# Delta-rule scan: level copies under a mask, and crossed row halves for the second unit of a group

## The chip, the cores and the metric

The program runs on one core of a Trainium2 chip. The metric is the device time of one execution in microseconds; the median of 3 runs of the kernel before is 5740.78 us (5734.3 to 5745.99).

## The reference

The program is a chain of blocks over 2048 tokens (plus 256 of context): a mixing block with a pooling branch, a delta-rule (RWKV) branch and a gated linear (HGRN) branch, and two attention blocks. The change concerns the delta-rule recurrence alone, which the reference computes token by token for 6 heads of 64 and 2 directions:

```python
def step(S, inp):
    w_t, k_t, v_t, kk_t, a_t = inp[:5]
    sa = jnp.einsum('bhvk,bhk->bhv', S, kk_t)
    S = (S * w_t[:, :, None, :] - sa[..., None] * (kk_t * a_t)[:, :, None, :]
         + v_t[..., None] * k_t[:, :, None, :])
    y = jnp.einsum('bhvk,bhk->bhv', S, inp[5]) if emit else None
    return S, y
```

The kernel computes it in chunks of 64 tokens. Within a chunk the recurrence is a triangular system, so a chunk needs the inverse of a unit triangular 64 × 64 matrix I − A; the state then moves from chunk to chunk with dense products.

## The kernel before

`rwkv_scan` (L1415 to L1740) is one stage of the program, with a barrier of all engines before and after it (`Scope.close`). It goes through 18 steps of 128 tokens, 2 of context and 16 that emit outputs. In a step there are 6 *units* (`u`: three pairs of heads times two directions) in 3 *groups* (`g`, two units each). A unit holds 128 tokens, two chunks of 64, each on one half of the 128 rows (`CHUNKS`), and two heads (`HEADS`). All loops are unrolled in Python, so TensorE's instructions are one long list.

A step has the phases of `PHASES` (L1428), and in each phase the three groups come in turn (`walk`, L1468):

- **z** and **n**, five levels of doubling (blocks of 2 up to 64). `W` holds the inverse so far and its transpose, started by GpSimd (L1535) from the identity plus level 0. In z (L1593 to L1597) TensorE multiplies the level's part of A with one of them and ScalarE copies the result to `K_Z` (L1683). In n (L1606 to L1613) TensorE multiplies that with the other, in both orders, and VectorE subtracts the products from `W` (L1715). The level's part of A comes from GpSimd, which multiplies A with six level masks `lv` for every unit (L1532). At level 1 the z phase also multiplies `K_KL` with `K_V` (L1599 to L1603).
- **x** (L1614): the inverse times two operands at once, 128 columns wide; ScalarE negates it into `X12` (L1686).
- **p** (L1621): the chunk's transition (`pq`) and its contribution and local output (`gram`), evacuated by VectorE (L1721) and ScalarE (L1689). The group's products for `pq` wait until VectorE has emptied `pq` of the group before, those for `gram` until ScalarE has.
- **f** and **s** (L1650): the state through the first and the second chunk, added up by VectorE (L1731, L1734).

Every matmul of z, n and x reads rows `t` (one chunk's half) and writes rows `t`:

```python
last = mm(d[t, at:at + HD], tk[t, K_LB + lev, u, HEADS[h]], wt[t, u, 0, HEADS[h]])
```

so unit 0 and unit 1 both use the array's quarters (rows 0, columns 0) and (rows 64, columns 64), and all their results lie in one PSUM bank per group (`db`, 512 columns). The products of p read rows `CHUNKS[cp]` and write rows `HEADS[h]` in the order of `LANES`, which visits all four quarters; `pq` and `gram` have two banks each, one for each row half read. `tb` is the bank of the transposes.

The work for the next step's units is put between the phases (`AHEAD`, L1429): after n of each of the five levels and after x, `front` (L1562) makes four transposes of a unit into `tb` (copied by ScalarE, L1676) and its 12 gram products into `gram` (multiplied by a mask into `TK`, VectorE, L1706). Before that GpSimd scales the unit's inputs (L1521, L1523). SP loads a unit's five arrays of the step after next with one DMA (L1495), in the p phase of the step that uses the buffer last, and stores outputs in s (L1501). The constants, the level masks among them, are loaded at the stage's start (L1481), and every engine waits for all five.

Of the kernel before, what the change touches and what calls it, by code (L numbers as in the profile page):

```python
# [1414 lines left out]
def rwkv_scan(nc, R, E, masks, levels, eye, ident, YR):  # L1415
# [8 lines left out]
    K_AL, K_BE, K_KA, K_V, K_A, K_AR, K_KL, K_KR, K_AT, K_LB, K_Z, K_W0 = 0, 1, 2, 3, 4, 5, 6, 7, 8, 9, 15, 16  # L1424
# [4 lines left out]
    AHEAD = {1: 0, 3: 1, 5: 2, 7: 3, 9: 4, 10: 5}  # L1429
# [3 lines left out]
    with ExitStack() as ctx:  # L1433
# [3 lines left out]
        TK = [[s.sb(f"TK{b}{g}", [P, 17, 2, P]) for g in range(NG)] for b in range(2)]  # L1437
# [6 lines left out]
        mk = s.sb("mk", [P, 2, 5, C])  # L1444
        lv = s.sb("lv", [P, 2, LV, P])
# [9 lines left out]
        xe_ready, tl_full, tl_done, gram_full, m4_done, lb_part, lb_ready = (  # L1455
            s.sem(n) for n in ("xe_ready", "tl_full", "tl_done", "gram_full", "m4_done", "lb_part", "lb_ready"))
# [11 lines left out]
        def walk(k, b, emit, phase, front):  # L1468

            nxt = after(k, b)  # L1470
            for i, (w, lev) in enumerate(PHASES):
                for g in range(NG):
                    phase(k, b, emit, w, lev, g)
                if nxt and i in AHEAD:
                    front(*nxt, AHEAD[i])

        with nc.Block() as block:
            @block.sync
            def _(sp):
                for dst, src in ((mk, masks), (lv, levels), (ey, eye), (idn, ident), (e, E)):  # L1480
                    sp.dma_start(dst[:], src).then_inc(const_in, 16)  # L1481
                for b in range(2):
                    for u in range(NU):
                        m, d = divmod(u, 2)
                        c = NLT + b if d == 0 else NS - 1 - b
                        sp.dma_start(X[b][u][:, X_AL:, :], R[c, m, d]).then_inc(x_in[b][u], 16)

                def step(k, b, emit):
                    if k < NLT // 2:
                        for u in range(NU):  # L1490
# [4 lines left out]
                            sp.dma_start(X[b][u][:, X_AL:, :], R[c, m, d]).then_inc(x_in[b][u], 16)  # L1495
# [12 lines left out]
            def _(pool):  # L1508
# [4 lines left out]
                def scaled(k, b, u):  # L1513
# [3 lines left out]
                    pool.wait_ge(x_in[b][u], k * 16 + 16)  # L1517
# [9 lines left out]
                def levels_of(k, b, u):  # L1527
# [4 lines left out]
                    nc.gpsimd.tensor_tensor(tk[:, K_LB:K_LB + LV, d, :], tk[:, K_A:K_A + 1, d, :].broadcast_to([P, LV, P]), lv[:, d, :, :],  # L1532
                                            ALU.mult).then_inc(lb_part, 1)
                    pool.wait_ge(lb_part, f + 1)
                    nc.gpsimd.tensor_tensor(W[b][g][:, d, :, :], tk[:, K_AT:K_LB + 1, d, :], ey[:].unsqueeze(1).broadcast_to([P, 2, P]),  # L1535
                                            ALU.add).then_inc(lb_ready, 1)

                def fronts(k, b):
                    scaled(k, b, 0)
                    scaled(k, b, 1)  # L1540
                    for u in range(NU):
                        levels_of(k, b, u)
                        if u + 2 < NU:
                            scaled(k, b, u + 2)
# [10 lines left out]
            def _(pe):  # L1555
# [6 lines left out]
                def front(k, b, u):  # L1562
# [3 lines left out]
                    begun = f > 0  # L1566
                    pe.wait_ge(xe_ready, f + 1)
                    if begun:
                        pe.wait_ge(tl_done, f)
                    for j, src in enumerate((x[:, X_AL, :], XE[u % 2][:, 0, :], XE[u % 2][:, 1, :], x[:, X_V, :])):  # L1570
                        t = nc.tensor.transpose(tb[:, j, :], src, idn[:])
                    t.then_inc(tl_full, 1)
                    if begun:
                        pe.wait_ge(m4_done, f)
                    for a, at in ((X_BE, 0), (X_KA, 2 * C)):
                        for cp, h in LANES:
                            mm(gram[CHUNKS[cp], h, at:at + 2 * C], x[HEADS[h], a, CHUNKS[cp]], x[HEADS[h], X_AL:X_RH + 1, CHUNKS[cp]])
                    for cp, h in LANES:
                        last = mm(gram[CHUNKS[cp], h, 4 * C:5 * C], x[HEADS[h], X_AL, CHUNKS[cp]], x[HEADS[h], X_BE, CHUNKS[cp]])
                    last.then_inc(gram_full, 1)  # L1580

                def phase(k, b, emit, w, lev, g):

                    tk, wt, d = TK[b][g], W[b][g], db[g]
# [2121 lines left out]
```

## Time and profile before

| | us |
|---|---|
| Median of 3 runs | 5740.78 |
| The profiled execution, its own time | 5741.89 |
| Its span, first to last instruction | 5740.1 |
| TensorE busy | 5142.9 |
| VectorE busy | 3334.5 |
| GpSimd busy | 1634.3 |

The profiled execution is 1.1 us above the median of the runs. Its span leaves 1.8 us of its own time outside. Busy times are for the whole program; the scan is the stretch from 1061 to 1857 us. In the rows, PE is TensorE's matmuls and PEld its weight loads, DVE VectorE, ACT ScalarE, POOL GpSimd, SP the engine that issues loads. An fp32 matmul leaves two records of each kind. "issue" is time in which an engine waited for nothing that the profile shows.

### The profile page before, as it was taken

The page shows a single profiled execution, that of the slowest core. Times are in us where ns is not written, and L with a number is a line of the kernel's source. Part 1 is how long each engine was busy: PE and PEld are TensorE (multiplying, and loading weights), DVE is VectorE, ACT ScalarE, POOL GpSimd, SP SyncE. Part 2 cuts the span into 40 slices and gives each one's busy share as a digit, 9 for nine tenths or more (in the row PEclk, how much of TensorE's full clock was granted, in tenths as well). Part 3 has the DMA queues.
Part 4 walks back from the last instruction along what each step waited for, and adds up shares of the span by engine and source line. Part 5 has one row for each costly group of instructions (what it writes and reads, how often), then busy time and mean ns, then how long its engine had stood idle before and what let it go on. Part 6 is the DMA issues. An engine that isn't in the chain of part 4 may idle for free. (4 is left out here: it accounts for less than half of the span.)

```text
span 5740.1 us, 122226 instructions
## 1 busy us (share of the span) xinstructions
PE 5142.9 (90%) x52673; PEld 3953.4 (69%) x52673; DVE 3334.5 (58%) x5037; ACT 1880.5 (33%) x3105; POOL 1634.3 (28%) x1351
## 2 busy tenths in 40 slices
PE   6899999899998786697999769999987999979989
PEld 1588888788888675485888534444466888766667
DVE  2237556344444777494995358888855100158877
ACT  1324444333332552224111314444412100126652
POOL 2201111444443441135000007777734311000012
PEclk8999999899999898898999879999998999979999
DMA  6334444312111112454332420000075211220035
GB/s 204 121 113 149 150 145 147 110 50 68 55 53 50 59 55 102 172 176 121 105 112 79 186 89 19 18 18 18 19 211 161 78 70 70 101 105 33 32 123 163
DMA packets 429687, 560.77 MB, mean 98 GB/s; under 512 B 66838, under 2 KB 318742, under 8 KB 417262
## 3 DMA queue, kind: packets, MB, share of 16 engines
q1 hardware_dynamic: 361480, 373.28, 21.0%
q10 hardware_dynamic: 52470, 122.50, 5.6%
q0 software_dynamic: 15216, 57.44, 2.5%
q8 instruction: 401, 6.57, 0.5%
q14 instruction: 120, 0.98, 0.1%
HBM read 350.00 MB, written 203.12 MB: 96 GB/s over the span
## 5 line engine op out<-in xcount | busy, mean ns | idle before, releaser
L157 PE MATMUL p_bank<-p_hT_high,p_w_high 128*128 128x512 f32 (+1 forms) x2744 | 1037.1, 378 | 7.9 <-PEq L37 7.9
L159 PE MATMUL p_bank<-p_hT_high,p_w_low 128*128 128x512 f32 (+1 forms) x2744 | 1028.9, 375 | 0.0
L158 PE MATMUL p_bank<-p_hT_low,p_w_high 128*128 128x512 f32 (+1 forms) x2744 | 1028.9, 375 | 0.0
L157 PEld LDWEIGHTS p_bank<-p_hT_high,p_w_high 128*128 128x128 f32 x2744 | 517.0, 188 | 110.1 <-issue 17.6
L159 PEld LDWEIGHTS p_bank<-p_hT_high,p_w_low 128*128 128x128 f32 x2744 | 516.8, 188 | 93.3
L158 PEld LDWEIGHTS p_bank<-p_hT_low,p_w_high 128*128 128x128 f32 x2744 | 517.2, 188 | 91.4
L2951 POOL TENSOR_TENSOR at_acc<-at_acc,at_p 128x512 f32<-128x512 f32 x256 | 415.1, 1622 | 122.8 <-ACT at_p L2887 99.8
L2887 ACT ACTIVATE at_p<-at_sc 128x1024 f32<-128x1024 f32 (+1 forms) x296 | 284.7, 1013 | 377.4 <-PE at_sc L2778 371.9
L1560 PE MATMUL rsc_db<-rsc_W,rsc_TK 64*64 64x64 f32 x8640 | 385.7, 220 | 4.6 <-issue 4.0
L2993 DVE TENSOR_REDUCE at_mx<-at_mb 128x2 f32<-128x1024 f32 (+1 forms) x280 | 342.1, 1222 | 50.7 <-PE at_mb L2789 50.4
L157 PE MATMUL o_bank<-o_w_high,o_m_high 128*128 128x512 f32 x800 | 314.7, 393 | 63.3 <-POOL o_m_low L151 63.3
L1560 PEld LDWEIGHTS rsc_db<-rsc_W,rsc_TK 64*64 64x64 f32 x8640 | 357.5, 137 | 5.2 <-issue 4.5
L158 PE MATMUL o_bank<-o_w_low,o_m_high 128*128 128x512 f32 x800 | 313.7, 392 | 0.0
L159 PE MATMUL o_bank<-o_w_high,o_m_low 128*128 128x512 f32 x800 | 313.5, 392 | 0.0
L1028 DVE COPY p_o<-p_bank 128x512 f32<-128x512 f32 (+1 forms) x52 | 33.8, 651 | 465.1 <-PE p_bank L159 465.1
L1715 DVE TENSOR_TENSOR rsc_W<-rsc_W,rsc_db 128x512 f32<-128x512 f32 x270 | 171.4, 635 | 208.8 <-PE rsc_db L1560 207.2
L1532 POOL TENSOR_TENSOR rsc_TK<-rsc_TK,rsc_lv 128x768 f32<-128x768 f32 x108 | 196.0, 1814 | 331.8 <-DVE rsc_TK L1706 331.8
L2810 PE MATMUL at_ob<-at_p,at_V 128*64 128x512 f32 (+1 forms) x1184 | 283.3, 599 | 0.7 <-ACT at_osb L2894 0.7
L1560 PE MATMUL rsc_db<-rsc_TK,rsc_W 64*64 64x64 f32 (+1 forms) x4320 | 258.4, 228 | 0.6 <-issue 0.6
L2777 PE MATMUL at_sc<-at_Q,at_K 128*128 128x512 f32 (+1 forms) x592 | 247.5, 419 | 1.8 <-DMA at_Q<-attention_tops 1.8
L406 ACT COPY p_o<-p_bank 128x512 f32<-128x512 f32 (+1 forms) x147 | 82.2, 560 | 476.7 <-PE p_bank L159 468.3
L3025 DVE TENSOR_TENSOR at_acc<-at_acc,at_p 128x512 f32<-128x512 f32 x256 | 204.2, 798 | 55.8 <-ACT at_p L2887 49.5
(428 smaller groups left out, 10401.2 us busy)
## 6 DMA issues: line engine op xcount, KB each, us to landing
rsc_X<-rwkv_chunks SPq DMA_DIRECT2D x108, 320.0 KB, 4.6
pT<-p_o ACTq DMA_DIRECT2D x128, 256.0 KB, 2.2
rwkv_chunks<-p_arr POOLq DMA_DIRECT2D x54, 512.0 KB, 5.4
o_z<-pT SPq DMA_DIRECT2D x50, 512.0 KB, 5.3
o_y<-y SPq DMA_DIRECT2D x50, 512.0 KB, 6.6
pT<-p_eo ACTq DMA_DIRECT2D x96, 256.0 KB, 2.0
x<-o_o ACTq DMA_DIRECT2D x32, 512.0 KB, 2.8
o_x<-x SPq DMA_DIRECT2D x32, 512.0 KB, 4.6
```

The costliest lines, as they stand in the source:

```text
L157: nc.tensor.matmul(out, lhs[0], rhs[0], start=start, stop=False)
L158: nc.tensor.matmul(out, lhs[0], rhs[1], start=False, stop=False)
L159: return nc.tensor.matmul(out, lhs[1], rhs[0], start=False, stop=stop)
L1532: nc.gpsimd.tensor_tensor(tk[:, K_LB:K_LB + LV, d, :], tk[:, K_A:K_A + 1, d, :].broadcast_to([P, LV, P]), lv[:, d, :, :], ALU.mult).then_i ...
L1560: return nc.tensor.matmul(out, l, r, start=start, stop=stop)
L1715: nc.vector.tensor_tensor(wt, wt, d[:].rearrange("p (u a t) -> p u a t", u=2, a=2)[:, :, lo:, :], ALU.subtract).then_inc(evac[g], 1)
L2777: nc.tensor.matmul(sc[t % 2][:, h, 0:n], K1[kv][:, keys], Q1[b % NBUF][:, h, 0:n], start=True, stop=False)
L2810: m = nc.tensor.matmul(ob[h * HD:(h + 1) * HD, 0:n], V[:, tiles[j], kv * HD:(kv + 1) * HD], pr[t % 4][:, h, 0:n], start=(j == 0), stop=(t ...
L2887: nc.scalar.activation(pr[t % 4][:, :, 0:n], sc[t % 2][:, :, 0:n], ACT.Exp, scale=SC).then_inc(exp_done, 1)
L2951: nc.gpsimd.tensor_tensor(acc[b % 2][:, 1, 0:n], acc[b % 2][:, 1, 0:n], pr[t % 4][:, 1, 0:n], ALU.add).then_inc(sum_b, 1)
L2993: r = nc.vector.reduce_max(mx[b % 2][:, :, t:t + nt, c], top_bank(m)[:, :, 0:nt * n].rearrange("p h (j k) -> p h j k", j=nt), AX)
L3025: nc.vector.tensor_tensor(acc[b % 2][:, 0, 0:n], acc[b % 2][:, 0, 0:n], pr[t % 4][:, 0, 0:n], ALU.add).then_inc(sum_a, 1)
```

## The change

- `K_A` gets a minus sign in the gram mask, and z multiplies the whole A with `W` in place of a level's part. What n makes is right only where the level's mask is set, so VectorE copies it into `W` under that mask (`copy_predicated`, the mask read as integers) in place of the subtraction. GpSimd's product with six levels goes; for unit 0 a product with level 0 remains, and unit 1 gets level 0 from four more gram products and a sixth mask.
- Unit 1 of a group has its rows crossed: its `X_AL` is loaded with the two token halves exchanged (two small DMAs beside the large one), so that its z reads rows `t` and writes the other half's rows, and the first half of n writes back. `rows_of` says which half.
- `db` becomes two banks for a group: in z and x a unit writes its own bank. `pq` and `tb` go; p's transition uses `db`, and the transposes use the first bank of `gram`. The eight banks are three times two and two.
- The loops of z, n, x go over heads outside and units inside, so that four matmuls in a row use four quarters.
- `front` is cut into `turned` (transposes) and `grams`, which now waits for ScalarE's copy, and both stand one phase earlier (the sixth unit's in n of level 5, the others' in the z phases; `turned` behind the first group, `grams` behind the third).

Core of the diff:

```diff
-    AHEAD = {1: 0, 3: 1, 5: 2, 7: 3, 9: 4, 10: 5}
+    AHEAD = {0: 0, 2: 1, 4: 2, 6: 3, 8: 4, 9: 5}
...
-        lv = s.sb("lv", [P, 2, LV, P])
+        lv = s.sb("lv", [P, LV, 2, 2, P])
...
-        pq = ctx.enter_context(nc.psum_tensor("rsc_pq", [P, 2, NT], F32))
-        db = [ctx.enter_context(nc.psum_tensor(f"rsc_db{g}", [P, NT], F32)) for g in range(NG)]
-        tb = ctx.enter_context(nc.psum_tensor("rsc_tb", [P, 4, P], F32))
+        db = [ctx.enter_context(nc.psum_tensor(f"rsc_db{g}", [P, 2, NT], F32)) for g in range(NG)]
...
             for i, (w, lev) in enumerate(PHASES):
                 for g in range(NG):
                     phase(k, b, emit, w, lev, g)
+                    if nxt and i in AHEAD and g == 0:
+                        turned(*nxt, AHEAD[i])
                 if nxt and i in AHEAD:
-                    front(*nxt, AHEAD[i])
+                    grams(*nxt, AHEAD[i])
...
+        def rows_of(u, t):
+            return t if u == 0 else other(t)
...
+                    sp.dma_start(x[:, X_RH:, :], src[:, 1:, :]).then_inc(x_in[b][u], 16)
+                    for t in CHUNKS:
+                        sp.dma_start(x[:, X_AL, other(t)], src[:, 0, t]).then_inc(x_in[b][u], 16)
...
-                    nc.gpsimd.tensor_tensor(tk[:, K_LB:K_LB + LV, d, :], tk[:, K_A:K_A + 1, d, :].broadcast_to([P, LV, P]), lv[:, d, :, :],
-                                            ALU.mult).then_inc(lb_part, 1)
+                    if d == 0:
+                        nc.gpsimd.tensor_tensor(tk[:, K_S0, d, :], tk[:, K_A, d, :], lv[:, 0, d, 0, :], ALU.mult).then_inc(s0_ready, 1)
...
+                def grams(k, b, u):
+                    pe.wait_ge(tl_done, f + 1)
...
+                    for cp, h in LANES if u % 2 else ():
+                        last = mm(gram[rows_of(u % 2, CHUNKS[cp]), h, 5 * C:6 * C], x[HEADS[h], X_BE, CHUNKS[cp]], x[HEADS[h], X_AL, rows_of(u % 2, CHUNKS[cp])])
...
-                        for u in range(2):
+                        for h in range(2):
+                            for u in range(2):
+                                for t in CHUNKS:
+                                    last = mm(d[rows_of(u, t), u, HEADS[h]], tk[t, K_A, u, HEADS[h]], wt[t, u, 1, HEADS[h]])
...
+                        for h in range(2):
+                            if lev < LV - 1:
+                                for u in range(2):
                                     for t in CHUNKS:
-                                        mm(d[t, at:at + HD], wt[t, u, 1, HEADS[h]], tk[t, K_Z, u, HEADS[h]])
-                                for t in CHUNKS:
-                                    last = mm(d[t, P + at:P + at + HD], tk[t, K_Z, u, HEADS[h]], wt[t, u, 1, HEADS[h]])
+                                        z, at = rows_of(u, t), 2 * P + 3 * P * u + h * HD
+                                        mm(flat[t, at:at + HD], wt[z, u, 0, HEADS[h]], tk[z, K_Z, u, HEADS[h]])
+                            for u in range(2):
+                                for z in CHUNKS:
+                                    at = 3 * P * u + h * HD
+                                    last = mm(flat[z, at:at + HD], tk[z, K_Z, u, HEADS[h]], wt[z, u, 0, HEADS[h]])
...
-                        if g:
-                            pe.wait_ge(evac[g - 1], done + 12)
...
-                        nc.vector.tensor_tensor(wt, wt, d[:].rearrange("p (u a t) -> p u a t", u=2, a=2)[:, :, lo:, :], ALU.subtract).then_inc(evac[g], 1)
+                        made_of = lv[:, lev, :, ways, :].bitcast(mybir.dt.uint32)
+                        new = d[:].rearrange("p b t -> p (b t)")[:, 0:6 * P].rearrange("p (u a t) -> p u a t", u=2, a=3)[:, :, 0::2, :]
+                        nc.vector.copy_predicated(W[b][g][:, :, ways, :], made_of, new[:, :, ways, :]).then_inc(evac[g], 1)
```

## Rows read from the trace of the kernel before

**Rows 1.** The page: the span, and part 1 (busy us, share, instructions).

```profile
span 5740.1 us, 122226 instructions
PE 5142.9 (90%) x52673; PEld 3953.4 (69%) x52673; DVE 3334.5 (58%) x5037; ACT 1880.5 (33%) x3105; POOL 1634.3 (28%) x1351
```

**Rows 2.** Windows: length, busy of PE, PEld, DVE, ACT, POOL, clock, DMA, GB/s.

```profile
1088.00:1857.00 769.00, 712.41 (x22648) 668.83 (x22640) 340.76 (x637) 235.62 (x480) 358.20 (x411) 0.98 0.17 53
1433.95:1466.47 32.52, 32.52 (x941) 31.00 (x943) 14.39 (x23) 11.43 (x24) 16.43 (x18) 0.96 0.05 12
1422.03:1433.95 11.92, 8.52 (x347) 7.52 (x341) 5.00 (x14) 1.85 (x4) 4.45 (x6) 0.96 0.56 179
```

**Rows 3.** Time line of one level: start, duration (us), engine, instructions.

```profile
1403.01 1.58 PE L1560 MATMUL rsc_db<-rsc_W,rsc_TK 64*64 64x64 f32 x48
1404.41 0.30 PE L1560 MATMUL rsc_db<-rsc_TK,rsc_W 64*64 64x64 f32 x4
1407.32 0.33 PE L1571 MATMUL rsc_tb<-rsc_idn,rsc_X 128*128 128x128 f32 x1
1407.91 0.78 PE L1560 MATMUL rsc_gram<-rsc_X 64*64 64x128 f32 x24
...
1408.51 1.58 PE L1560 MATMUL rsc_db<-rsc_W,rsc_TK 64*64 64x64 f32 x48
...
1408.02 0.59 ACT L1676 COPY rsc_TK<-rsc_tb 128x512 f32<-128x512 f32 x1 [3.01 <-PE rsc_tb L1571]
```

**Rows 4.** Time line of TensorE in the x and p phases of that step.

```profile
1418.11 2.80 PE L1560 MATMUL rsc_db<-rsc_TK,rsc_W 64*64 64x128 f32 x48
...
1423.32 0.30 PE L1560 MATMUL rsc_gram<-rsc_X,rsc_TK 64*64 64x64 f32 x8
1423.43 0.30 PE L1560 MATMUL rsc_gram<-rsc_TK 64*64 64x64 f32 x8
```

**Rows 5.** DMA queues in 1088 to 1857 us: packets, MB, share of 16 engines.

```profile
q8 instruction: 177, 2.90, 1.6%
```

**Rows 6.** Waits of TensorE in 1088 to 1857 us: total, times, longest.

```profile
PE rsc_db L1560 <- issue: 30.8, 19, 3.1
```

**Rows 7.** Windows between two waits on issue; and 21 us of a later stage.

```profile
1823.60:1827.90 4.30, 3.94 (x127) 3.80 (x127) 0.91 (x4) 1.76 (x3) 0.00 (x0) 1.00 0.33 93
...
2199.00:2220.00 21.00, 20.75 (x769) 19.51 (x768) 15.13 (x36) 6.43 (x13) 3.24 (x3) 1.00 0.08 30
1518.80:1522.65 3.85, 3.85 (x127) 3.80 (x128) 0.62 (x2) 1.52 (x3) 0.00 (x0) 1.00 0.35 99
...
1782.50:1786.60 4.10, 3.92 (x129) 3.84 (x129) 0.00 (x0) 1.76 (x3) 0.00 (x0) 1.00 0.24 65
```

**Rows 8.** Time line of TensorE behind two waits (idle before, what ended it).

```profile
1827.91 0.27 PE L1560 MATMUL rsc_db<-rsc_TK,rsc_W 64*64 64x64 f32 x1 [0.37 <-issue]
...
1432.94 0.37 PE L1560 MATMUL rsc_db<-rsc_PQ,rsc_S 64*64 64x64 f32 x2 [2.15 <-issue]
```

**Rows 9.** Windows in the state part, the second after its long wait.

```profile
1428.00:1430.00 2.00, 2.00 (x94) 2.00 (x87) 0.58 (x2) 0.59 (x1) 1.90 (x4) 1.00 0.98 338
...
1434.00:1436.00 2.00, 2.00 (x44) 2.00 (x42) 0.70 (x3) 0.00 (x0) 0.00 (x0) 0.50 0.16 41
```

**Rows 10.** Groups of the scan by line: busy us, mean ns, idle before.

```profile
L1532 POOL TENSOR_TENSOR rsc_TK<-rsc_TK,rsc_lv 128x768 f32<-128x768 f32 x108 | 196.0, 1814 | 331.8 <-DVE rsc_TK L1706 331.8
...
L1715 DVE TENSOR_TENSOR rsc_W<-rsc_W,rsc_db 128x512 f32<-128x512 f32 x216 | 148.7, 688 | 188.7 <-PE rsc_db L1560 188.7
L1706 DVE TENSOR_TENSOR rsc_TK<-rsc_gram,rsc_mk 128x640 f32<-128x640 f32 x108 | 89.1, 825 | 144.7 <-PE rsc_gram L1560 144.7
```

**Rows 11.** Groups of VectorE in the stage behind the scan, by line and form.

```profile
L2036 DVE TENSOR_TENSOR hg_P<-hg_sc,hg_mk 128x768 f32<-128x768 f32 x94 | 89.0, 947 | 0.0
...
L2015 DVE TENSOR_TENSOR hg_qe<-hg_qe,hg_f 128x512 f32<-128x512 f32 x11 | 21.2, 1927 | 7.1 <-ACT hg_lv L1940 7.1
```

**Rows 12.** Window of the scan's first loads.

```profile
1061.00:1068.00 7.00, 0.00 (x0) 0.00 (x0) 0.00 (x0) 0.00 (x0) 0.68 (x5) 0.50 0.89 291
```

More of the change, by code:

```diff
@@ L1466, in after, with walk @@
             return None if k == NLT // 2 and b == 1 else ((k, 1) if b == 0 else (k + 1, 0))
-        def walk(k, b, emit, phase, front):
+        def walk(k, b, emit, phase, turned, grams):
             nxt = after(k, b)
@@ L1662, in phase @@
                                     at = u * P + cp * HD
-                                    last = mm(d[q, at:at + HD], S[n][g][q, u, :], PQ[g][q, u, cp, 1, :])
+                                    last = mm(d[q, 0, at:at + HD], S[n][g][q, u, :], PQ[g][q, u, cp, 1, :])
                     last.then_inc(prod[g], 1)
                 for u in range(NU):
-                    front(0, 0, u)
-                scan(lambda k, b, emit: walk(k, b, emit, phase, front))
+                    turned(0, 0, u)
+                    grams(0, 0, u)
+                scan(lambda k, b, emit: walk(k, b, emit, phase, turned, grams))
             @block.scalar
@@ L1672, in _, with turned @@
                 act.wait_ge(const_in, 16 * 5)
-                def front(k, b, u):
+                def turned(k, b, u):
                     act.wait_ge(tl_full, k * (2 * NU) + (b * NU + u + 1))
-                    nc.scalar.copy(TK[b][u // 2][:, K_AL:K_V + 1, u % 2, :], tb[:]).then_inc(tl_done, 1)
+                    nc.scalar.copy(TK[b][u // 2][:, K_AL:K_V + 1, u % 2, :], gram[:, 0, :].rearrange("p (a t) -> p a t", a=4)).then_inc(tl_done, 1)
                 def phase(k, b, emit, w, lev, g):
@@ L1691, in _ @@
                 for u in range(NU):
-                    front(0, 0, u)
-                scan(lambda k, b, emit: walk(k, b, emit, phase, front))
+                    turned(0, 0, u)
+                scan(lambda k, b, emit: walk(k, b, emit, phase, turned, lambda k, b, u: None))
             @block.vector
@@ L1738, in _ @@
                 for u in range(NU):
-                    front(0, 0, u)
-                scan(lambda k, b, emit: walk(k, b, emit, phase, front))
+                    grams(0, 0, u)
+                scan(lambda k, b, emit: walk(k, b, emit, phase, lambda k, b, u: None, grams))
 def hgrn(nc, PT, q0, i0, z0, masks, ident, head_ones, YH):
@@ L3649, in constants @@
         small = lv[0:HD, d, 0:6, 0:HD].copy()
[L3650 to L3652 removed]
+        c["rwkv_masks"][:, d] = np.tile(np.stack([-1.0 * strict, incl, strict, incl, -small[:, 0].T, -small[:, 0]], 1), (2, 1, 1))
+        for way, x in enumerate((small, small.transpose(2, 1, 0))):
+            c["rwkv_levels"][:, :, d, way] = np.tile(x, (2, 1, 2))
     c["eye_64"] = np.tile(np.eye(HD, dtype=f), (2, 2))
```

114 lines of the change are left out of this document (58 added, 56 removed).

## The prediction

> **What bounds the kernel now.** I read the page first: TensorE is busy for 90% of 5740.1 us, its weight loads for 69% [rows 1]. That is a mean over many stages, and the change touches one of them, the delta-rule scan, which is closed off from its neighbours by a barrier, so whatever the scan gains or loses moves the end one for one.
>
> The stretches come next. The 18 steps of the scan fill 1088 to 1857 us: 769.0 us, 42.7 us a step, and TensorE is busy for 712.4 of them, VectorE for 340.8 [rows 2]. One step, cut in two: from its first level product to its p phase 32.52 us (call it the level part), and from p to the next step's first product 11.92 us (the state part) [rows 2].
>
> The time line of one level shows what the level part is made of [rows 3]. Level n starts at 1403.01, its z products end and the n products start at 1404.41, the next unit's transposes start at 1407.32, its grams at 1407.91, the next level at 1408.51: 5.50 us, with TensorE never waiting. A z phase is 48 records (an fp32 matmul leaves two), 1.40/48 = 29.2 ns each; n is 96 records, at that rate 2.8 of the 2.91 us between its start and the transposes. These products use only the two diagonal quarters of the array (rows t to columns t). The p phase already walks all four: 8 records start every 0.12 us [rows 4], 14.6 ns each. So on the array crossed row halves are worth a factor of two, and this kernel shows it.
>
> The second thing to see is the instruction queue. In the 769 us TensorE executed 22648 matmuls and 22640 weight loads, and 177 packets of 16 KB came in on the instruction queue [rows 2, 5]: 256 instructions a packet, a packet every 4.34 us. Some waits of TensorE on "issue", 30.8 us in 19 pieces [rows 6], have the spacing of packets: between two of them lie 127 or 128 matmuls and as many loads, and the stretches took 3.85, 4.10 and 4.30 us at full clock [rows 7], the last ended by a wait of 0.37 us on "issue" [rows 8]. Six packets' worth (769 matmuls) ran at 3.50 us a packet in a later stage [rows 7]. I read this as a supply: a packet costs 3.5 to 4.3 us, and TensorE can't run faster than that for long. In the state part it is worse, because the chunk loads fill the DMA engines (share 0.98) and the next packet comes late: 2.15 us of waiting [rows 8, 9].
>
> **The change, part by part.**
>
> *Crossed halves.* z (5 levels) and the K_KL·K_V products that go with level 1 fall from 1.40 to 0.70 us each: 6 × 0.70 = 4.2 us a step. In n the first half of each group of products is spread over four quarters, the second half stays on the diagonal, so the diagonal carries three of four former turns: 2.8 becomes 2.1, on four levels 2.8 us (level 5 has only the diagonal half). x is 48 records in 2.80 us, 58 ns each, double width [rows 4], and halves: 1.4 us. Together 8.4 us of array time a step.
>
> *What it adds on TensorE.* Odd units get four more gram products: 12 matmuls, 24 records at 14.6 ns = 0.35 us, and 48 instructions a step. The transposes now land in the gram bank, so the grams wait until ScalarE has copied them. That copy starts 0.70 us after the transposes begin and takes 0.59 [rows 3]; behind the transposes only two z groups (2 × 0.23 us) cover it, so TensorE stands about 0.3 us, five times a step. The sixth unit's transposes wait for VectorE's mask of the fifth (0.83 us and the way there and back, against 0.47 us of cover): some 0.6 us. Behind each of these waits stand the products of the next groups. On ScalarE the z copies of groups 1 and 2 now queue behind that copy; their n products stand 0.7 and 1.4 us further down TensorE's order, so nobody waits for them. The front work of each unit starts one phase earlier, so the first unit's scaled inputs are asked for after the step's first z group; GpSimd makes them in the state part, and I count nothing. Sum added: 0.35 + 1.5 + 0.6 = 2.45 us, and an array that needs 32.52 − 8.4 + 2.45 = 26.6 us for the level part.
>
> *What the supply allows.* The level part holds 941 + 943 instructions [rows 2], with the 48 new ones 1932, or 7.55 packets. At 3.5 us a packet 26.4 us, at the mean of the three measured stretches (4.08) 30.8 us. I take 3.8, between the quiet stretch and the scan's own, since the level part has little other DMA (share 0.05): 28.7 us. The supply is longer than the array, so it sets the pace, and the added waits of 2.45 us lie beside it. Gain: 32.52 − 28.7 = 3.8 us a step, 18 × 3.8 = 68 us. The state part is held by packets and chunk loads already; I count nothing for the wait on the neighbour's bank that p loses, nor for the shorter wait on the mask.
>
> *Level copies under a mask.* VectorE's subtraction on 512 elements out of PSUM is 688 ns [rows 10]. No predicated copy runs in the kernel before. It reads a mask and PSUM and writes the same 512 elements; nearest row, the same 688. Bounds: below, a cheaper copy gains nothing, since it is hidden already; above, the dearest VectorE instruction of 512 elements that I found in the trace, 1927 ns [rows 11]. At 688 VectorE has 3 × 0.69 + 0.96 = 3.0 us of work in a level, under the 5.2 us that the level would take; the work stays hidden and costs nothing. It is uncovered above (5.2 − 0.96)/3 = 1.4 us an instruction. The odd mask grows from 640 to 768 elements (825 to 947 ns [rows 10, 11]), counted in the 0.96.
>
> *GpSimd* loses the six-level product, 1814 ns a unit [rows 10], and gets a small one for even units. It is off the path: nothing gained. *Queues:* SP issues three loads in place of one for odd units, six more a step, two of them in 256-byte pieces; the buffer is read a step later, so this is hidden, but it can lengthen the stretch in which packets come late. The pieces carry a fifth of an odd load, a tenth of all; the DMA engines are filled for 0.56 of 11.92 us in the state part [rows 2], 6.7 us, and if that tenth took twice as long it would be 0.7 more. So 0 to 0.7 us in each of 16 steps with loads; I take 0, the nearest case being the same bytes on the same queue, and keep 11 us for the far end. *Start:* the level table doubles from 0.79 to 1.57 MB (by its shape) ahead of everything, at 291 GB/s [rows 12]: +2.7 us.
>
> Sum: 5741.9 (the profiled execution; the median of the runs shown is 1.1 lower) − 68 + 2.7 = 5676.
>
> By the Trainium skill ("TensorE: Matmul & The Clock Gate", Part 1, "Wait — 56ns, not 53.3ns?") matmuls never start closer than about 25 ns however small they are; by that a z phase would shrink only to 48 × 25 = 1.2 us, and the array would gain 1.2 us on z and K_KL·K_V in place of 4.2. The trace does not agree: 14.6 ns in the p phase [rows 4].
>
> **The rivals.**
>
> *The supply is no limit* (packets can come faster when asked for faster; the fastest stretch, 3.50, had no wait in it and may be demand alone). Then the array decides: 18 × (32.52 − 26.6) = 107 us: 5741.9 − 107 + 2.7 = 5638, and up to 18 × 1.3 = 23 us less, 5615, if the wait of 0.6 us and half of the five of 0.3 find cover. Against it: the waits with a packet's spacing in stretches without chunk loads [rows 7, 8].
>
> *Nothing comes of it.* Packets stay at the pace they have now (1884 instructions in 32.52 us is 4.42 us a packet), or the crossed quarters don't overlap when both units of a row half write two banks. For it: the state part's packets take that long already. Time: 5741.9 + 2.7 and up to 11 more, 5745 to 5756.
>
> *VectorE becomes the bound*, in the copy under a mask. At 1927 ns a level takes 0.96 + 3 × 1.93 = 6.7 us against 5.5 now: 4 × 1.2 × 18 = 89 us lost, 25 regained in x: about 5809. It decides from 1.5 us an instruction, where a level reaches today's 5.5. For it: a third stream (the mask) beside PSUM. Against it: the same form with two streams is 688. By the Trainium skill ("TensorEngine Tiling (Array Packing)", "PSUM Bottleneck") evacuation may become the limit once tiles run four at a time. The rows give VectorE 3.0 of 5.2 us, so here that needs the dearer copy.
>
> A slower clock would act the same way in small: after a long wait the granted clock is 0.50 for some us [rows 9], the lower of its two levels. At that clock four-quarter records come at twice 14.6 ns, 3.7 us a packet, still within the supply, so I price it at nothing.
>
> **How the numbers follow.** Supply-bound (5676; 5638 to 5714 between 3.5 us a packet, where the array decides, and 4.08) 0.58; no supply limit (5638) 0.22; nothing 0.11; slower through VectorE or a wait that I missed 0.09. About 0.2% (11.5 us) is what a measurement of this kernel can tell from no change. The range takes in the first two cases whole, from 5615 to the end of what counts as a gain, 5730, and leaves out the last two, 0.20. Faster 0.58 + 0.22 = 0.80; same 0.11; slower 0.09.
>
> **What would show it.** Right: z in 0.70 us; 16 KB packets nearer 3.8 us apart all through the level part, with TensorE waiting on "issue" about 0.5 us once a packet; VectorE's copies at about 0.69; a step near 39 us. Wrong towards faster: packets well under 3.5 us apart and "issue" small. Wrong towards slower: TensorE waiting on the copies of VectorE, or copies above 1.4 us; z still at 1.40 would say that the quarters don't overlap.

## The result and the profile after

The changed kernel takes 5710.26 us (median of 4 runs, 5688.31 to 5711.63), the kernel before 5743.39 us in the same comparison: ratio 0.9943, 95% interval 0.9923 to 0.9963. Two later comparisons of the same pair, on two chips, gave 0.9927 (0.991 to 0.9944) and 0.992 (0.9906 to 0.9934). So it is faster by 33 to 46 us, where 65 was forecast.

The page of the profiled execution (5688.31 us) beside [rows 1]:

```profile
span 5686.5 us, 123108 instructions
PE 5037.7 (89%) x53105; PEld 3828.1 (67%) x53105; DVE 3339.5 (59%) x5037; ACT 1863.1 (33%) x3105; POOL 1460.6 (26%) x1297
```

Windows, columns as in [rows 2]: the 18 steps, then one level part and the state part behind it:

```profile
1090.56:1799.50 708.94, 602.77 (x23050) 541.98 (x23044) 346.09 (x637) 218.50 (x480) 194.38 (x358) 0.99 0.20 57
...
1408.47:1437.65 29.18, 25.96 (x965) 23.30 (x961) 15.74 (x25) 9.62 (x23) 8.80 (x17) 1.00 0.07 18
1437.65:1448.85 11.20, 9.23 (x341) 8.60 (x337) 3.92 (x12) 2.68 (x5) 2.60 (x5) 0.85 0.61 179
```

The rows of PE and PEld count records, two of each kind for a product. The steps fell from 769.0 to 708.9 us, 60 us in all. TensorE's busy time fell by 110 us, so 50 of the 110 came back as waiting. The waits of TensorE in the 18 steps, beside [rows 6], say on what:

```profile
PE rsc_db L1586 <- issue: 60.1, 80, 2.1
PE rsc_gram L1586 <- issue: 19.4, 26, 1.8
PE rsc_gram L1596 <- DVE rsc_TK L1738: 9.1, 17, 0.6
...
PE rsc_db L1586 <- DVE rsc_W L1748: 0.6, 2, 0.4
```

In these two groups "issue" holds 79.5 us in 106 pieces. The instruction queue brought 180 packets in these 709 us, one in 3.94 us, where [rows 5] had one in 4.34:

```profile
q8 instruction: 180, 2.95, 1.8%
```

The time line of TensorE in one level, beside [rows 3]:

```profile
1334.51 0.39 PE L1586 MATMUL rsc_db<-rsc_W,rsc_TK 64*64 64x64 f32 x6 [0.99 <-issue]
...
1335.47 0.33 PE L1596 MATMUL rsc_gram<-rsc_idn,rsc_X 128*128 128x128 f32 x1
1335.64 0.38 PE L1596 MATMUL rsc_gram<-rsc_idn,rsc_XE 128*128 128x128 f32 x2
...
1336.06 0.69 PE L1586 MATMUL rsc_db<-rsc_W,rsc_TK 64*64 64x64 f32 x32
1336.81 0.90 PE L1586 MATMUL rsc_gram<-rsc_X 64*64 64x128 f32 x32
```

The z products of groups 1 and 2, 32 records, take 0.69 us from the first start to the last end; without the length of the last (0.22 us for a lone record) 0.47 us from the first start to the last, 15.2 ns a record. Halves do cross at about the rate of the p phase. The grams start 0.75 us behind the first of these products, and so 0.28 us behind the last: they wait for ScalarE's copy, which ends at 1336.76. The rows of PE don't show this wait, because the record before it is drawn 0.22 us long. Those of the weight loads do; the last row is their sum over the 18 steps:

```profile
1336.17 0.59 ACT L1707 COPY rsc_TK<-rsc_gram 128x512 f32<-128x512 f32 x1 [0.17 <-PE rsc_gram L1596]
1336.80 0.76 PEld L1586 LDWEIGHTS rsc_gram<-rsc_X 64*64 64x64 f32 x32 [0.19 <-ACT rsc_TK L1707]
...
PEld rsc_gram L1586 <- ACT rsc_TK L1707: 9.4, 50, 0.2
```

VectorE, beside [rows 10]:

```profile
L1748 DVE COPY_PREDICATED rsc_W<-rsc_lv,rsc_db 128x512 f32<-128x512 uint32 x216 | 150.7, 735 | 37.6 <-PE rsc_db L1586 37.0
L1738 DVE TENSOR_TENSOR rsc_TK<-rsc_gram,rsc_mk 128x768 f32<-128x768 f32 x52 | 49.8, 958 | 72.7 <-PE rsc_gram L1586 72.7
```

On 512 elements the copy under a mask takes 735 ns where the subtraction took 688, the larger mask 958 where 947 was taken, and TensorE waits 0.6 us for the copy in all 18 steps.

I cut both traces at the first z and the first p product of each step and counted TensorE's instructions. The large gaps stand behind the same instruction of every 256; I call them packet waits. They are counted from the start of one record to the start of the next, so each is some 0.2 us longer than in the rows of waits. Means of 17 steps: level part 32.22 us before (0.22 of packet waits) and 29.61 after (3.99); state part 11.01 (2.35) and 10.18 (2.09). The scan's start, from its first instruction to the first z, took 27.5 us and now takes 34.6. Here is TensorE's time line of it:

```profile
1065.96 0.44 PE L1596 MATMUL rsc_gram<-rsc_idn,rsc_X 128*128 128x128 f32 x1 [14.55 <-POOL rsc_XE L1549]
...
1067.78 1.35 PE L1586 MATMUL rsc_gram<-rsc_X 64*64 64x128 f32 x24 [0.74 <-ACT rsc_TK L1707]
1070.16 0.45 PE L1596 MATMUL rsc_gram<-rsc_idn,rsc_X 128*128 128x128 f32 x1 [1.04 <-DVE rsc_TK L1738]
```

Transposes, copy, grams and mask of a unit now go through one bank, one after the other: 4.2 us from one unit's transposes to the next's. Before, the transposes had `tb`, and a unit took 3.5 us. The first transposes also start later, 10.0 us after the stage's first instruction in place of 7.9.

### The profile page after: what moved, and what is told of

It reads as the page before. It is cut to its first block and busy times, and to the rows that moved or that the text cites. A ratio compares the mean times of both kernels' runs of the same rounds, so it can differ in the third digit from the quotient of the medians.

```text
span 5686.5 us, 123108 instructions
## 1 busy us (share of the span) xinstructions
PE 5037.7 (89%) x53105; PEld 3828.1 (67%) x53105; DVE 3339.5 (59%) x5037; ACT 1863.1 (33%) x3105; POOL 1460.6 (26%) x1297
## 5 line engine op out<-in xcount | busy, mean ns | idle before, releaser
L1586 PE MATMUL rsc_db<-rsc_W,rsc_TK 64*64 64x64 f32 x8640 | 298.5, 223 | 28.8 <-issue 27.4
L1586 PEld LDWEIGHTS rsc_db<-rsc_W,rsc_TK 64*64 64x64 f32 x8640 | 258.4, 135 | 53.1 <-issue 51.2
L2810 PE MATMUL at_sc<-at_Q,at_K 128*128 128x512 f32 (+1 forms) x592 | 247.7, 419 | 2.0 <-DMA at_Q<-attention_tops 2.0
L2811 PE MATMUL at_sc<-at_Q,at_K 128*128 128x512 f32 (+1 forms) x592 | 232.3, 393 | 0.0
L1738 DVE TENSOR_TENSOR rsc_TK<-rsc_gram,rsc_mk 128x640 f32<-128x640 f32 x108 | 96.3, 891 | 228.4 <-PE rsc_gram L1586 228.4
L157 PEld LDWEIGHTS o_bank<-o_w_high,o_m_high 128*128 128x128 f32 x800 | 151.9, 190 | 97.7 <-POOL o_m_low L151 66.1
```

The costliest lines, as they stand in the source:

```text
L157: nc.tensor.matmul(out, lhs[0], rhs[0], start=start, stop=False)
L1586: return nc.tensor.matmul(out, l, r, start=start, stop=stop)
L1738: nc.vector.tensor_tensor(dst, src, mk[:, u % 2, 0:items, :].unsqueeze(1).broadcast_to([P, 2, items, C]), ALU.mult).then_inc(m4_done, 1)
L2810: nc.tensor.matmul(sc[t % 2][:, h, 0:n], K1[kv][:, keys], Q1[b % NBUF][:, h, 0:n], start=True, stop=False)
L2811: m = nc.tensor.matmul(sc[t % 2][:, h, 0:n], K2[kv][:, keys], Q2[b % NBUF][:, h, 0:n], start=False, stop=True)
```

## The experiments

**The pair again.** The kernel before, profiled once more, and the changed kernel twice, unedited.

> The kernel before, unedited, profiled once more. Its first profiled execution took 5741.9 us, but on the chip of the last runs 17 executions lay between 5714 and 5742 with a median of 5731. If the first profile was a slow one among many, this one is near 5731 and has steps of about 42.5 us in place of 43.2, the difference in the state part (its wait once in 256 instructions, 2.35 us a step, is the only large one that can vary). If the chip makes the difference, all runs here agree within 10 us and the step is the same from profile to profile.

> The changed kernel once more, unedited. Its profiled execution took 5688.3 us and its three other runs 5709.8 to 5711.6. If the profiled one was simply one end of what this kernel does from run to run, the new profiled execution and the five timed runs fall anywhere between 5685 and 5715. If there is something that profiled executions have and timed ones not, the profile is near 5688 again and the timed runs near 5710. In the scan: a level part of about 29.6 us with about 4 us of it in waits at the instruction index where the last trace had them (one in 256), a state part of about 10.2 us, first z about 34.6 us after the stage begins.

> The changed kernel once more, as the measure for the run beside it on the same chip: ratio to the kernel before 0.9920 to 0.9945, level part 29.3 to 29.7 us, state part 10 to 10.3 us, first z 34.5 to 35 us after the stage begins.

Before: profiled 5733.3 us, level 31.96, state 10.53 us, so steps of 42.5 us, as expected. Changed: profiled 5684.2 and 5690.1 us, timed medians 5686.3 and 5684.7; level 29.36 and 29.61, state 9.97 and 9.75, first z after 35.0 and 35.6 us. So a profiled execution is like any other, and [rows 1] came from a run some 8 us above the usual. The changed kernel's 5710 us of the first comparison did not come again; I can name no cause for it.

**Fewer instructions, the same columns.** In z:

```diff
-                        for h in range(2):
-                            for u in range(2):
-                                for t in CHUNKS:
-                                    last = mm(d[rows_of(u, t), u, HEADS[h]], tk[t, K_A, u, HEADS[h]], wt[t, u, 1, HEADS[h]])
+                        for u in range(2):
+                            for t in CHUNKS:
+                                last = mm(d[rows_of(u, t), u, 0:P], tk[t, K_A, u, HEADS[0]], wt[t, u, 1, :])
```

> Leaves out the second head's products in z: a unit's chunk is one product of 128 columns with the first head's A in place of two of 64 columns. The columns that pass through the array stay the same, the instructions of z halve: 3 groups x 5 levels x 4 products fewer, 240 instructions a step, 0.94 packets of 256. Theory one (TensorE is paced by the supply of instructions in the level part): the waits once in 256 instructions, 4.0 us a step in the level part, shrink by some 3 us, the level part goes from 29.6 to about 26.5 us, and the kernel is 45 to 65 us faster than the changed kernel on the same chip. Rival (the array or the waits on copies pace it, and the waits on issue are only where they are booked): the columns are the same, so 0 within 10 us.

Median 5642.4 us, 43.9 under the changed kernel on the same chip, just short of the 45 to 65. Its waits in the 18 steps:

```profile
PE rsc_db L1586 <- issue: 29.2, 34, 1.9
PE rsc_gram L1586 <- issue: 13.0, 14, 1.7
```

42 us of issue in place of 79.5; level part 27.1 us, packet waits in it 1.6. What is left without these waits, 25.5 us, is what the changed kernel's level part has left (29.6 - 4.0 = 25.6). The columns are the same and the time isn't: in the level part, TensorE was short of instructions.

**More instructions.** Each z product cut into two of 32 columns.

```diff
-                                    last = mm(d[rows_of(u, t), u, HEADS[h]], tk[t, K_A, u, HEADS[h]], wt[t, u, 1, HEADS[h]])
+                                    for q in (0, 32):
+                                        half = slice(h * HD + q, h * HD + q + 32)
+                                        last = mm(d[rows_of(u, t), u, half], tk[t, K_A, u, HEADS[h]], wt[t, u, 1, half])
```

> The z products of the changed kernel (not those of K_KL and K_V) cut into two of 32 columns each: the same columns, 240 instructions a step more, 0.94 packets. Theory one (supply): the level part takes 0.94 x 3.8 = 3.6 us a step more, 29.5 to about 33, the packet waits in it stay at 4 us or grow, and the kernel is 50 to 70 us slower than the changed one, slower than the kernel before by 5 to 25 us. Rival (the array sets the pace): the columns are the same, so less than 20 us slower.

Median 5818.9 us, ratio to before 1.0144 (1.013 to 1.0159): by the ratios 115 to 129 us slower than the changed kernel, where 50 to 70 were expected. I had counted wrongly: 8 products more in each of 15 phases are 480 instructions, 1.88 packets, and at 3.8 us that is 7.1 us a step. Measured 36.0 - 29.5 = 6.5, and the packet waits rose to 7.1 us. It is no clean test, because the array pays too: 30 records of 32 columns take as long as 30 of 64,

```profile
1371.09 0.66 PE L1586 MATMUL rsc_db<-rsc_W,rsc_TK 64*64 64x32 f32 x30
```

so between 32 and 64 columns time goes by records here. (It does not between 64 and 128: in [rows 4] a record of 128 columns takes 58 ns, twice the 29.2 of one of 64.)

**The supply alone.** TensorE walks a list of products with nothing around it (64 products are one packet). In place of the program stand calls of `run(n, quarters, columns)`; the first kernel's come first, then the second's:

```diff
+                run(64 * 16, two, 128).then_inc(part, 1)
+                run(64 * 16, two, 64).then_inc(part, 1)
+                run(64 * 16, four, 64).then_inc(part, 1)
+                run(64 * 16, four, 16).then_inc(part, 1)
+                run(64 * 24, four, 16).then_inc(part, 1)
+                for i in range(6):
+                    run(128, two, 128)
+                    run(128, four, 16)
...
+                run(64 * 16, four, 64).then_inc(part, 1)
+                run(64 * 16, four, 32).then_inc(part, 1)
+                for i in range(4):
+                    run(256, two, 128)
+                    last = run(256, four, 64)
+                last.then_inc(part, 1)
+                run(64 * 24, four, 64)
```

> Leaves out the whole program: TensorE alone walks a list of fp32 products (rows 64, columns of weights 64) in seven stretches, the output is zeros. Packets of 256 instructions hold 64 products. By the records of the scan a packet's demand on the array is 7.5 us (two quarters, 128 columns), 3.7 us (two quarters, 64), 1.9 us (four quarters, 64), under 1.9 us (four quarters, 16); then 24 packets of the last kind beside loads that fill the DMA engines; then two packets of the first kind and two of the fourth in turn, six times. Theory (one packet is asked for when the one before it is entered, and is there about 3.5 to 3.7 us later): the packets come 7.5, 3.7 to 3.8, 3.4 to 3.7 and 3.4 to 3.7 us apart, with the loads 4.5 to 6.5 us, and in the last stretch the slack of the slow packets isn't saved up: the quick ones still take 3.4 us or more each, a pair of pairs 2 x 7.5 + 2 x 3.5 = 22 us. Rival one (no such limit; the chunks of the scan were slow for another reason): the third and fourth stretch run at their demand, under 2 us a packet. Rival two (packets are fetched several ahead): the third and fourth as in the theory, but in the last stretch a pair of pairs takes 2 x 7.5 + 2 x 2 = 19 us or less.

> Leaves out the whole program, as the last run of this kind; TensorE alone, the output is zeros. Stretches: 16 packets of four quarters with 64 columns; 16 packets of four quarters with 32 columns; four times four packets of two quarters with 128 columns (7.0 us a packet in the last run) and four of four quarters with 64 (2.09 us); 24 packets of four quarters with 64 columns beside loads that fill the DMA engines. Theory (one packet ahead, so slack isn't saved): the first stretch 3.5 to 3.7 us a packet with 1.4 to 1.6 us of waiting in each; in the third, the first boundary between two quick packets behind slow ones already has a wait of about 1.4 us, as all others have. Rival (several packets are fetched ahead): behind the slow packets the first one or more boundaries between quick packets have no wait. Second stretch: if a record costs 14.6 ns however narrow it is, 2.0 to 2.1 us of work a packet as in the first; if time goes by columns, 1.0. Last stretch: 6 us a packet, as with the 16 columns of the last run, if the loads set it; under 4 us if it was the lower clock there (0.50).

Four quarters, 64 columns (first kernel):

```profile
190.53 2.09 PE L98 MATMUL sup_ps<-sup_A 64*64 64x64 f32 x128 [1.36 <-issue]
193.99 2.09 PE L98 MATMUL sup_ps<-sup_A 64*64 64x64 f32 x128 [1.36 <-issue]
197.72 2.09 PE L98 MATMUL sup_ps<-sup_A 64*64 64x64 f32 x128 [1.64 <-issue]
```

128 records, which is a packet, are done in 2.09 us, and then TensorE waits: a packet every 3.45 or 3.73 us, seldom 4.0. The 16 columns ran at a granted clock of 0.50, the lower of the two levels, and needed 3.6 us of work a packet, so that stretch and the last one settled nothing. The second kernel did:

```profile
153.75 2.09 PE L98 MATMUL sup_ps<-sup_A 64*64 64x64 f32 x128 [1.36 <-issue]
157.21 2.09 PE L98 MATMUL sup_ps<-sup_A 64*64 64x64 f32 x128 [1.36 <-issue]
160.66 31.90 PE L98 MATMUL sup_ps<-sup_A 64*64 64x64 f32 x768 [1.36 <-issue]
193.71 2.09 PE L98 MATMUL sup_ps<-sup_A 64*64 64x64 f32 x128 [1.15 <-issue]
...
341.93 3.54 PE L98 MATMUL sup_ps<-sup_A 64*64 64x64 f32 x128 [2.95 <-issue]
348.14 3.35 PE L98 MATMUL sup_ps<-sup_A 64*64 64x64 f32 x128 [2.67 <-issue]
```

Behind slow packets (7.0 us each, up to 147.1 us) and one that holds both kinds, the first whole packet of quick records follows without a wait, at 150.3 us, and the next one, at 153.75, is waited for as the others are. In the later rounds that wait is some 0.2 us shorter (1.15 us at 193.71 against 1.36). So packets that took 7 us buy next to nothing for later, as if one were fetched ahead and no more. The last two lines are beside loads that fill the DMA engines (window, columns without VectorE and ScalarE):

```profile
300.00:390.00 90.00, 49.03 (x1843) 46.49 (x1836) 0.00 (x0) 0.63 1.03 394
```

There a packet costs 6.2 us (348.14 - 341.93), as it did in the first kernel with 16 columns beside loads (6.2 us at 3.6 us of work), so the loads set it.

**Straight rows.** `rows_of` returns `t` for every unit, and loads and grams follow; contrary to what I wrote, that leaves nothing of the computation out.

```diff
-            return t if u == 0 else other(t)
+            return t
```

> The odd units' rows are not crossed (each reads and writes its own half; loads go to straight halves), all else as in the changed kernel, so what the odd units compute is wrong: both units of a group use the two diagonal quarters. Theory (four quarters halve z, x and a part of n): array time of the level part returns from 25.6 us (29.6 less 4.0 of packet waits) to about 25.6 + 8.4 = 34 us, the packet waits in it go to about 0, z takes 1.40 us again, and the kernel is (34 - 29.6) x 18 = about 80 us slower than the changed one. Rival (the crossing brought little, and the gain is from the copies under the mask and GpSimd): within 15 us of the changed kernel.

Median 5735.1 us (12 runs), 48.8 slower than the changed kernel, ratio to before 1.0007 (0.9996 to 1.0017). So the crossing is the whole gain: copies under a mask, new banks and earlier fronts come to nothing together. They do so by parts that cancel: a mean level part of 33.13 us and a first z after 34.4 us lose what the state part, 9.23 us in place of 10.5 to 11.0, gains. The crossing was expected to be worth some 80 us. One level part, with one of 29.18 us above:

```profile
1263.98:1296.12 32.14, 31.55 (x964) 30.11 (x963) 16.32 (x25) 10.80 (x23) 9.69 (x18) 1.00 0.11 32
```

TensorE is busy for all but 0.6 us. The mean level part has 0.6 us of packet waits, so the array needs 32.5; crossed it needs 25.6. Of 6.9 us that the array saves a step, the supply takes 3.4 back in the level part, and about 1.0 in the state part, where the packet waits are 1.1 us with straight rows and 2.1 crossed.

**The order of the products.** Crossing kept, unit outside and head inside again in z, n and x, as here in z:

```diff
-                        for h in range(2):
-                            for u in range(2):
+                        for u in range(2):
+                            for h in range(2):
```

> The crossing as in the changed kernel, but the products of z, n and x in the order of the kernel before (unit outside, head inside), so that two quarters in a row are used twice before the other two. Theory (only products that stand next to each other in the list overlap): z takes about 1.2 to 1.4 us again, the array time of the level part is 30 to 33 us, its packet waits fall under 1.5 us a step, and the kernel is 20 to 50 us slower than the changed one. Rival (the array looks far enough ahead, or the supply of instructions covers it): z stays at 0.70 us, and the time within 8 us of the changed kernel.

Ratio 0.9939 (0.9926 to 0.9952), within the changed kernel's own three (0.992 to 0.9943). That kernel didn't run beside this one or the two of the next experiment, so differences under some 13 us can't be told there. The z products of two groups:

```profile
1306.23 0.74 PE L1586 MATMUL rsc_db<-rsc_W,rsc_TK 64*64 64x64 f32 x32
```

0.74 us against 0.69. The rival holds: products needn't stand next to each other to overlap. The time line of n shows records of later products between those of earlier ones: in the list four records of each kind (`TK,W`, then `W,TK`) follow each other in turn, but six of the first kind start before the second's.

```profile
1307.69 0.30 PE L1586 MATMUL rsc_db<-rsc_TK,rsc_W 64*64 64x64 f32 x4
1307.81 0.30 PE L1586 MATMUL rsc_db<-rsc_W,rsc_TK 64*64 64x64 f32 x4
1307.93 0.30 PE L1586 MATMUL rsc_db<-rsc_TK,rsc_W 64*64 64x64 f32 x6
1308.04 0.22 PE L1586 MATMUL rsc_db<-rsc_W,rsc_TK 64*64 64x64 f32 x1
```

**The loads.** Four of a step's six moved into the z phases of the next step; and, in another kernel, odd units with one load.

```diff
-                            if d == 0:
-                                sp.wait_ge(evac[m], k * (2 * EVACS) + (b * EVACS + 12))
+                        else:
+                            sp.wait_ge(evac[0], (n + 1) * EVACS + 2 * u - 3)
```

```diff
-                    if u % 2 == 0:
+                    if u >= 0:
                         sp.dma_start(x[:, X_AL:, :], src).then_inc(x_in[b][u], 16)
```

> The changed kernel with four of a step's six unit loads moved from the p phase into the z phases of the levels 1 to 4 of the next step, one unit at a time; same bytes, same queue. Theory (in the state part the instruction packets come late because the loads fill the DMA engines): the wait once in 256 instructions in the state part falls from 1.9 to 2.1 us a step to about 1, in the level part it stays within 0.5 us of 3.6 to 4.0, and the kernel is 10 to 18 us faster than the changed one. Rival (a packet costs what it costs and the loads only move where it is late): the level part loses what the state part gains, 0 within 6 us.

> Odd units are loaded with one DMA as in the kernel before, so their X_AL isn't crossed and what they compute from it is wrong; all instructions of TensorE, VectorE and ScalarE stay. It prices the two loads in 256-byte pieces, which the prediction bounded by 0 and 0.7 us in each of 16 steps. If the pieces lengthen the state part: its packet wait falls by 0.3 to 0.7 us a step and the kernel is 5 to 11 us faster than the changed one (ratio to before 0.9910 to 0.9918). If they cost nothing: within 4 us of it (0.9927 on the chip of the first runs).

Ratios 0.9931 (0.9917 to 0.9945) and 0.9942 (0.993 to 0.9954): no gain by either that shows. Spread, the packet waits went from 1.9 - 2.1 to 1.75 us in the state part and from 3.6 - 4.0 to 4.3 in the level part, and a step took 39.5 us where the changed kernel's took 39.3 to 39.8. That fits the rival, that the cost moves along with the loads, but the differences are small. The 256-byte pieces cost nothing that shows, as forecast: with one load the state part was no shorter (11.2 us).

**The start.** In two attempts. The first gave the transposes banks of their own; the second also put two units of transposes ahead of the grams, let GpSimd scale all units first and loaded the tables after the first inputs.

```diff
-                for u in range(NU):
-                    turned(0, 0, u)
-                    grams(0, 0, u)
+                for u in range(NU + 2):
+                    if u < NU:
+                        turned(0, 0, u, db[u // 2][:, u % 2, :])
+                    if u > 1:
+                        grams(0, 0, u - 2, True)
...
-                for dst, src in ((mk, masks), (lv, levels), (ey, eye), (idn, ident), (e, E)):
+                for dst, src in ((ey, eye), (idn, ident), (e, E)):
```

> Only ahead of the first step: the six units' transposes go to the six banks of the level products, which are idle there, in place of one after another through the gram bank, and a unit's transposes come before the grams of the unit before it. Theory (the start of the scan lost 7.1 us to the chain transposes, copy, grams, mask, one unit after the other, 4.2 us a unit against 3.5 before): a unit takes 2.9 us, the first z comes 27 to 28.5 us after the stage begins in place of 34.6, and the kernel is 6 to 8 us faster than the changed one. Rival (the start waits for the larger level table or for GpSimd): first z still after 33 us and no gain.

> The changed kernel with another start: the first loads are what the first units need (the level table and the masks come later, with waits of their own), GpSimd scales all six units ahead, and the six units' transposes go into the idle banks of the level products, two units ahead of the grams. Theory (the start lost 7 us to a table twice as large ahead of everything and to a chain through one bank): first z comes 25 to 28 us after the stage begins in place of 34.6 to 35, and the kernel is 7 to 10 us faster than the changed one (against the kernel before: about 0.7 + 0.15 = 0.85%). Rival (the start hides behind something that I have not seen): first z earlier but less than 3 us gained.

> The changed kernel with the other start once more, beside the changed kernel on the same chip. First z came 22.2 us after the stage begins in place of 34.6, yet the time was only some 7 us under what the changed kernel's ratio gives. If the 12 us earlier start is worth 12 us and the rest was the chip, this run is 10 to 13 us faster than the changed kernel beside it; if the first step gives back what the start gains (its first level waits for GpSimd's W or for loads), 5 to 8 us, and the first step is longer than the others by the difference.

The first: first z after 37.4 us, 5684.5 us, 1.8 under the changed kernel, where 6 to 8 were expected. In its order a unit's transposes, which wait for GpSimd, stood ahead of the grams of the unit before. The second ran on two chips. On the first of them: first z after 22.2 us, 5678.9 us, ratio to before 0.99 (0.9887 to 0.9913), without the changed kernel beside it. On the other: first z after 22.3 us (1085.24 - 1062.91, the scan's first instruction),

```profile
1083.90 1.56 PE L1595 MATMUL rsc_gram<-rsc_X 64*64 64x128 f32 x32 [0.95 <-DVE rsc_TK L1755]
1085.24 0.65 PE L1595 MATMUL rsc_db<-rsc_W,rsc_TK 64*64 64x64 f32 x16
```

and 5668.1 us beside 5684.7 for the changed kernel on the same chip, ratio to before 0.989 (0.9874 to 0.9905). That is 16.6 us, more than either case expected. Some 13 us come from the start. In the two profiles the stage, from its first instruction to its last, takes 739.0 and 727.3 us, 11.7 apart, so the rest lies outside the scan, where the code is the same. Of the kernels that leave nothing out it is the fastest.

## Why the prediction was right and wrong

Right were the direction, the mechanism and most prices: z in half its time, the copy at 735 ns where 688 was taken (it would have mattered above 1.4 us), GpSimd and the small loads all but free (TensorE waits 3.0 us for GpSimd in the 18 steps, in two pieces), a step near 39 us (39.3 to 39.8), and TensorE waiting for instructions (forecast "about 0.5 us once a packet"; measured 3.99 us in 7.53 packets, 0.53). The array came to 25.6 us where 26.6 was worked out. VectorE as the bound and "nothing comes of it" are refuted. The range, which took in two cases whole, holds all medians of the changed kernel (5684.7 to 5710.3).

Wrong was the size. By terms, forecast against the two first profiles:

| | forecast us | measured us |
|---|---|---|
| Level part | 18 x (32.52 - 28.7) = -68 | 18 x (32.22 - 29.61) = -47 |
| State part | 0 | 18 x (11.01 - 10.18) = -15 |
| Start | +2.7 | 34.6 - 27.5 = +7.1 |
| Sum | -65 | -55 (the two executions differ by 53.6) |

Two steps were at fault in the largest term, "Gain: 32.52 − 28.7 = 3.8 us a step". The 32.52 us were one step's, and the mean was 32.0 to 32.2: 5 to 10 us. And "I take 3.8", a packet's price, measured 29.61 / 7.53 = 3.93, another 16 us. Behind that stands the sentence "The supply is longer than the array, so it sets the pace": I compared the two sums. But next to nothing is saved from one packet to the next, so each packet costs the longer of its own two. Of 110 whole packets in the level parts, 82 ended in a wait and came 3.80 us apart, the price forecast; 28 had no wait and took 4.03, because their own products needed that long. A mean demand of 3.38 us and a supply of 3.5 to 3.8 thus made 3.86. That is less than half of the 16 us. The larger part lies ahead of the first packet boundary of a level part, where 129 instructions take 2.63 us on average, or 5.2 us a packet; why they do was not tested.

"Start: +2.7" counted the table's bytes and not the chain. The bytes may be the 2.1 us by which the first transposes start later (10.0 us in place of 7.9). The other 5.0 us are the chain of a unit through one bank. I had priced its waits inside a step and not ahead of the first step, where nothing covers them. Inside a step the price was right: the grams' wait for ScalarE's copy, priced at 0.3 us five times a step, is 0.27 us from start to start, behind four units of the six.

The state part, counted at nothing, gained 0.8 us a step: 0.3 in packet waits and 0.5 in a wait that moved. The sixth unit's wait on VectorE's mask was sized right, 9.1 us in 17 waits, 0.54 against 0.6, but it isn't new. In the kernel before, the first group's products for `gram` in p waited for the same mask, in the state part of every step:

```profile
PE rsc_gram L1560 <- DVE rsc_TK L1706: 8.6, 17, 0.5
```

In the changed kernel that row is gone. The prediction added the wait where it arrives and took nothing off where it leaves ("nor for the shorter wait on the mask").

The sum of the profiles, 54 us, is still above the timed 33 to 46. Some 8 us of that is the first profile of the kernel before, which took longer than usual; I had noted it as 1.1 above a median of three runs, which was too few. From its first instruction to its last the stage took 798.2 us before, and 785.5 in the second profile; changed it took 745.5, 737.2 and 739.0. Against 785.5 the gain is 40 to 48 us, as in the two later comparisons; the 33 us of the first stay open.

By the Trainium skill ("TensorE: Matmul & The Clock Gate", Part 1, "Wait — 56ns, not 53.3ns?") matmuls don't start closer than about 25 ns. The trace does not agree where quarters differ: 15.2 ns a record in z. What the runs do show of that kind is that 30 records of 32 columns take 0.66 us, no less than as many of 64.

## What to carry to other kernels

Count instructions as a resource of their own. Where TensorE got through 256 of them (here 64 small fp32 products) in less than 3.5 to 3.8 us, faster products bought little and fewer, wider ones bought time; and since next to nothing was saved from packet to packet, compare packet by packet and not in sums. A chain that other work nearly covers in the steady state stands bare in the first pass: price the prologue separately. And a wait that a change moves is to be added at one place and taken off at the other.

## What was not expected of the hardware

- A packet of quick instructions cost 3.45 or 3.73 us with no other loads under way, and 6.2 us beside loads at 394 GB/s, with 16 columns as with 64.
- The order in the list hardly matters across quarters: four products in a row on two quarters hardly held up those for the other two (0.74 against 0.69 us).
- In the second list TensorE's granted clock was 1.00 with 64 columns, busy for 28.6 of 50 us, and mostly the lower level with 32 columns, on the same quarters and with as many products a packet; no run here shows why:

```profile
10.00:60.00 50.00, 28.61 (x1763) 26.74 (x1754) 0.00 (x0) 1.00 0.02 5
62.00:110.00 48.00, 44.57 (x1664) 43.55 (x1660) 0.00 (x0) 0.53 0.02 4
```
